# First block's rotary embedding: the halves of queries and keys exchanged by DMA within SBUF instead of by a matrix product

## The reference, cut to what matters

```
def apply_rope(x, cos, sin):
    x1, x2 = jnp.split(x.astype(jnp.float32), 2, axis=-1)
    ...
    return jnp.concatenate([x1 * c - x2 * s, x2 * c + x1 * s], axis=-1)

for l in range(DEPTH):                       # DEPTH = 2
    ...
    q = apply_rope(rms_norm(q.reshape(bsz, seq, 16, 64), q_norm_g[l]), cos, sin)
    k = apply_rope(rms_norm(k.reshape(bsz, seq, 16, 64), k_norm_g[l]), cos, sin)
    ...
    iq, ik = apply_rope(iq, cos, sin), apply_rope(ik, cos, sin)
    o_attn = dsa_attention(q, k, v, iq, ik, iw, n_keep) @ w_attn_o[l]
    xs, bm, cm = ...                         # convolution, state-space scan (ssd_scan), 32 heads
    ...
```

## Time and profile before

| What | Value |
|---|---|
| median of 3 runs | 2268.84 us (2265.83 to 2271.03) |
| the profiled execution's own time | 2264.96 us |
| its span, first to last instruction | 2263.2 us |
| TensorE busy | 2153.4 us, 95% of the span |
| VectorE busy | 1664.1 us, 74% |
| ScalarE busy | 1409.4 us, 62% |
| TensorE clock granted, mean | 0.993 of full speed |

### The profile page before, as it was taken

How to read it: one execution, slowest core, us unless ns; L and a number is a source line. 1 busy time by engine, 2 the same in 40 slices (tenths; PEclk the granted TensorE clock), 3 DMA queues, 4 the chain that set the end, 5 groups by cost and what they waited for, 6 DMA issues and landing times.

```text
span 2263.2 us, 42342 instructions
## 1 busy us (share of the span) xinstructions
PE 2153.4 (95%) x17416; PEld 2062.9 (91%) x17416; DVE 1664.1 (74%) x3018; ACT 1409.4 (62%) x2206; POOL 180.6 (8%) x170
## 2 busy tenths in 40 slices
PE   2989999999999899999999999899999999999999
PEld 1978899999999788999999999799999998899999
DVE  5898778678868987786678875757788784657654
ACT  2678897456546778974665456964654656764542
POOL 0000000022100000000124100000030110000000
PEclk9999999999999999999999999999999999999999
DMA  7545556657656555466565531545655422455663
GB/s 281 197 159 185 176 168 225 204 179 240 234 190 200 157 183 180 165 224 205 167 197 161 185 113 56 159 145 179 190 187 186 158 88 91 145 158 166 187 191 125
DMA packets 110593, 395.26 MB, mean 175 GB/s; under 512 B 12320, under 2 KB 13888, under 8 KB 110272
## 3 DMA queue, kind: packets, MB, share of 16 engines
q1 hardware_dynamic: 96768, 344.09, 47.1%
q0 software_dynamic: 11904, 43.03, 5.9%
q10 hardware_dynamic: 1728, 5.43, 0.6%
HBM read 391.46 MB, written 1.05 MB: 173 GB/s over the span
## 4 chain that ended last, share of the span: by engine, by line
PE 72%; ACT 12%; DVE 11%; issue 3%; DMA 2%; SPq 0%; ACTq 0%; DVEq 0%
PE bank L553 71%; ACT scr L1086 3%; ACT WH L1086 3%; DVE WL L1636 3%; ACT L1075 3%; ACT arena L1086 2%; DVE arena L1732 2%; DMA ring<-in_w 2%; DVE arena L2405 1%; DVE scr L1928 1%; DVE scr L1715 1%; DVE scr L1915 1%; DVE small L1927 0%; PE bank L637 0%; DVE scr L2001 0%
## 5 line engine op out<-in xcount | busy, mean ns | idle before, releaser
L1086 ACT ACTIVATE WH<-ring 128x1024 fp32r<-128x1024 f32 (+1 forms) x638 | 669.0, 1052 | 685.1 <-PE bank L553 660.7
L553 PE MATMUL bank<-HTH,WH 128*128 128x256 f32 (+1 forms) x3408 | 974.4, 286 | 13.5 <-DVE HTL L1705 4.7
L553 PE MATMUL bank<-HTL,WH 128*128 128x256 f32 (+1 forms) x3408 | 959.5, 282 | 0.0
L553 PE MATMUL bank<-HTH,WL 128*128 128x256 f32 (+1 forms) x3408 | 959.3, 281 | 0.0
L1636 DVE TENSOR_TENSOR WL<-ring,WH 128x1024 fp32r<-128x1024 f32 (+2 forms) x610 | 739.0, 1220 | 167.7 <-ACT WH L1086 165.0
L553 PEld LDWEIGHTS bank<-HTH,WH 128*128 128x128 f32 (+1 forms) x3408 | 643.3, 189 | 26.0 <-issue 7.8
L553 PEld LDWEIGHTS bank<-HTL,WH 128*128 128x128 f32 (+1 forms) x3408 | 643.4, 189 | 2.6 <-issue 2.1
L553 PEld LDWEIGHTS bank<-HTH,WL 128*128 128x128 f32 (+1 forms) x3408 | 643.2, 189 | 0.1
L1075 ACT ACT_TABLE_LOAD x119 | 152.7, 1283 | 22.1 <-DMA arena<-in_crow 13.4
L553 PE MATMUL bank<-ff2h,WH 128*128 128x256 f32 x512 | 143.8, 281 | 0.0
L553 PE MATMUL bank<-ff2l,WH 128*128 128x256 f32 x512 | 143.8, 281 | 0.0
(11 more groups left out here) (333 smaller groups left out, 3593.0 us busy)
## 6 DMA issues: line engine op xcount, KB each, us to landing
ring<-in_w SPq DMA_DIRECT2D x620, 512.0 KB, 4.1
arena<-in_wada POOLq DMA_DIRECT2D x80, 512.0 KB, 4.8
ring<-in_w SPq DMA_DIRECT2D x24, 384.0 KB, 3.3
arena<-in_wada SPq DMA_DIRECT2D x8, 512.0 KB, 19.2
arena<-in_wada ACTq DMA_DIRECT2D x8, 512.0 KB, 21.8
XT<-in_xt SPq DMA_DIRECT2D x1, 1024.0 KB, 9.0
arena<-in_s POOLq DMA_DIRECT2D x4, 256.0 KB, 3.7
ring<-in_w SPq DMA_DIRECT2D x8, 128.0 KB, 2.0
```

The source lines that it names most:

```text
L553: ins = e.matmul(out, a, b, start=(start and i == 0), stop=(stop and i == len(pairs) - 1))
L1086: return e.activation(out, a, func, **kw)
```

## The change

The permutation product of the eight rotary steps is gone from PE. Instead SP issues four DMAs for each of the eight, SBUF to SBUF: each moves a block of 32 partitions of queries and keys (2 rows of 512 fp32 in a partition, 128 KB) to the neighbouring block of 32 partitions in the lane's scratch tiles. SP issues them ahead of the load of the unit that lies 8 past the unit of step 11 or 22, after a wait on DVE's `gain`. DVE waits for all four and multiplies the scratch tiles in place. The sign goes from the matrix into the sine table (one more ACT instruction of 128x256 at the start); the permutation products of the indexer's queries and keys stay. The timetable changes: the step that takes up the exchanged halves comes three units after the gain and not two, and the steps behind it are one unit later until the next place where they meet the old numbers.

```diff
@@ timetable
-    "attn0": [5, 7, 9, 11, 13, 15, 17, 19, 21, 23, 25, 27, 29, 31, 33, 35, 39, 41, 43, 45, 47, 51, 53, 55, 57, 59, 61,
-              63, 65, 67, 69, 71],
-    "attn1": [5, 7, 9, 11, 13, 15, 18, 20, 22, 24, 31, 33, 35, 37, 39, 41, 43, 45, 47, 49, 51, 55, 57, 59, 61, 63, 65,
-              67, 69, 71, 73, 75],
+    "attn0": [5, 7, 9, 11, 13, 15, 17, 19, 21, 23, 25, 27, 30, 32, 34, 36, 39, 41, 43, 45, 47, 51, 53, 56, 58, 60, 62,
+              64, 66, 68, 70, 72],
+    "attn1": [5, 7, 9, 11, 13, 15, 18, 20, 22, 24, 31, 33, 36, 38, 40, 42, 44, 46, 48, 50, 52, 55, 57, 60, 62, 64, 66,
+              68, 70, 72, 74, 76],
@@ SyncE
+            exchanges = {plan.base[2 * l] + A_TICKS["attn%d" % par][slot] + 8: (l, par, bi)
+                         for l in range(2) for par in range(2) for bi, slot in ((par, 11), (par + 2, 22))}
             for x in units:
+                if x.i in exchanges:
+
+                    l, par, bi = exchanges[x.i]
+                    p.wait_ge((LA, LB)[par].V("gain", l, bi))
+                    for b in range(4):
+                        to, of = slice(32 * b, 32 * b + 32), slice(32 * (b ^ 1), 32 * (b ^ 1) + 32)
+                        e.dma_start(scr[to, 2 * par:2 * par + 2, :], QK[of, :, 512 * bi:512 * bi + 512]).then_inc(
+                            swapped[par].inc(*((l, bi) if b == 3 else ()), by=16), 16)
@@ TensorE
-                p.wait_ge(L.V("gain", l, bi))
-                mm(L.b[0][0:n, :], [(perm, xq)])
-                mm(L.b[1][0:n, :], [(perm, xk)]).then_inc(L.P.inc("turn", l, bi), 1)
@@ VectorE
-                p.wait_ge(L.P("turn", m, bi), L.V("gain", m, bi))
+                p.wait_ge(swapped[L is LB](m, bi), L.V("gain", m, bi))
                 for i, x in enumerate((xq, xk)):
-                    e.tensor_tensor(v2(s[i]), v2(b[i]), twice(sinap), ALU.mult).then_inc(L.V.inc(), 1)
+                    e.tensor_tensor(v2(s[i]), v2(s[i]), twice(sinap), ALU.mult).then_inc(L.V.inc(), 1)
@@ ScalarE, at the start
+            act(trig[:, 1, :], trig[:, 1, :], ACT.Identity, scale=con("sgn")).then_inc(start_scalar.inc(), 1)
```

More of the change, by code:

```diff
@@ L41 @@
 CONSTS = [("id", 128), ("ones", 128), ("blk", 128), ("perm", 128), ("dup", 64), ("tri0", 256),
-          ("mask", 256), ("rot", 256), ("scan", 256), ("invf", 1), ("eps", 1), ("same", 32)]
+          ("mask", 256), ("rot", 256), ("scan", 256), ("invf", 1), ("eps", 1), ("sgn", 1), ("same", 32)]
 def const_columns():
@@ L66, in const_array @@
         if m % 64 < 32:
-            put["perm"][m + 32, m] = -1
+            put["perm"][m + 32, m] = 1
         else:
@@ L83, in const_array @@
     put["eps"][:] = 1e-6
+    put["sgn"][:] = np.where(p % 64 < 32, -1, 1)
     return c
@@ L362, in program @@
         cst = sb("cst", [128, NCON])
-        cols = sb("cols", [128, NCOL + 30])
+        cols = sb("cols", [128, NCOL + 29])
         rows = sb("rows", [128, 128])
@@ L420, in program @@
         XCL, XCH = over("xcl", oXC, 16), over("xch", oK, 16)
+        QK = ar(0, 2, 2048)
         adabuf, silc = ar(oADA, 1024), ar(oSC, 1024)
@@ L476, in program @@
         opened = sig("opened")
+        swapped = [sig("swapped_a"), sig("swapped_b")]
         FREED_BY_VECTOR = {"su", "xc", "ao", "so", "res", "up", "pe", "b0", "b1", "b2"}
@@ L600, in attn @@
                 for bi in (par, par + 2):
-                    yield from rope_pe(L, l, bi, flat(Q[:, 2 * bi:2 * bi + 2, :]), flat(K[:, 2 * bi:2 * bi + 2, :]),
-                                       con("blk"), con("perm"), 128)
+                    yield
+                    p.wait_ge(L.A("sq", l, bi))
+                    mm(L.b[0][:, :], [(con("blk"), L.s[0])])
+                    mm(L.b[1][:, :], [(con("blk"), L.s[1])]).then_inc(L.P.inc("ss", l, bi), 1)
+                    yield
+                    yield
                     for pr in (2 * bi, 2 * bi + 1):
@@ L608, in attn @@
                                            lambda h, t: VV[:, t, 64 * h:64 * h + 64], ev_scalar("v", l, 3, 2 * l))
-            def rope_pe(L, l, bi, xq, xk, ones, perm, n):
-                yield
-                p.wait_ge(L.A("sq", l, bi))
-                mm(L.b[0][0:n, :], [(ones, L.s[0][0:n, :])])
-                mm(L.b[1][0:n, :], [(ones, L.s[1][0:n, :])]).then_inc(L.P.inc("ss", l, bi), 1)
-                yield
-                p.wait_ge(L.V("gain", l, bi))
-                mm(L.b[0][0:n, :], [(perm, xq)])
-                mm(L.b[1][0:n, :], [(perm, xk)]).then_inc(L.P.inc("turn", l, bi), 1)
-                yield
             def pair_pe(L, l, pr, before, bi, q, k, v, v_ready):
@@ L1594, in scalar_program @@
             p.wait_ge(start_vector("angle"))
-            act(trig[:, 1, :], x, ACT.Sin).then_inc(start_scalar.inc(), 1)
+            act(trig[:, 1, :], x, ACT.Sin).then_inc(start_scalar.inc("sine"), 1)
+            p.wait_ge(in_cst("in"), start_scalar("sine"))
+            act(trig[:, 1, :], trig[:, 1, :], ACT.Identity, scale=con("sgn")).then_inc(start_scalar.inc(), 1)
             act(y, x, ACT.Abs).then_inc(start_scalar.inc("abs"), 1)
@@ L1843, in rope_dve @@
             def rope_dve(L, m, bi, xq, xk, gq, gk, cosap, sinap, n):
-                s, b = [t[0:n, :] for t in L.s], [t[0:n, :] for t in L.b]
+                s = L.s
                 yield
```

## The result

The changed kernel is slower: median 2278.86 us (2275.97 to 2281.54, five executions) against 2268.84 us of the kernel before on the same chip (2265.83 to 2272.08), ratio 1.0043, 95% interval 1.0028 to 1.0057. Its profiled execution has a span of 2274.2 us, 11.0 us more than before; the granted clock is 0.989 on average, before 0.993. The forecast was 2264.4 us, a gain of 4.4 us.

A forecast was written before the change was run, and what follows sets the result against it. TensorE, busy 95% of the span, was taken to set the pace. A layer, 0.64 - 0.1 + 1.81 - 0.35 + 0.2 = 2.2 us, twice gives 4.4 of 14.7: 2268.84 - 4.4 = 2264.4 us, range 2256 to 2270.5.

The forecast's parts named there:

- fourth step: Units 59 to 62: wins of 1.72, 0.46 and 0.27 against a wait of 2.8, net -0.35 us a layer.
- pays 2.8: Unit 62: TensorE stands before `qk` at S + 6.9, keys come at S + 9.7, a 2.8 us wait.
- small waits that end: Units 64 to 76: attention in even units, scan in odd ones spreads ScalarE's work, winning 0.2 us a layer.
- first step: Unit 29: the scan's `y` needs VectorE's decays, so only 0.64 us come back and 1.3 become a wait.
- second step: Units 33 to 38: 1.1 us won, then lost to a 1.2 us wait for `attn1`'s keys; net -0.1 us.
- What is removed: Four permutation products a layer on TensorE: 7.35 us a layer, 14.7 for both, the most removal alone can give.
- Third step: Unit 55: no clump, `attn0` alone in unit 56, so the whole 1.81 us are won.
- Between and behind: Units 64 to 76, behind the fourth step: a win of 0.2 us a layer from small waits that end.
- second rival: Full ScalarE holds up even-unit steps, table changes in units 64 and 68: gain 0.4 us, 2268.4; chance 0.15.
- third rival: Late transfer, deciding from 8.5 us after the first step's gain; landing after 12 us gives 2273.6; chance 0.13.
- The Trainium skill's estimate: Exchange transfer: 1.3 + 2.0 + 2.4 = 5.7 us at half the ports, against 5.1 by the rows; hidden either way.
- forecast of 115 table loads: ScalarE's table loads fall by four in the new order, 5.1 us, to 115; not what the path waits for.

The follow-up runs named there:

- e1: The kernel before with only the new timetable, the permutation products staying on TensorE: 2281.17 us against 2267.80, ratio 1.0062.
- e14: The changed kernel with five idle products ahead of the wait for pair 6's keys in unit 62, a repeat run: 2272.57 us, ratio 1.0022.
- e9: Exchange by DMA on the old timetable with only the gains earlier, the first in unit 26: 2261.21 us against 2267.42 of the kernel before, ratio 0.9973.
- e10: The kernel before with an idle 64-column product ahead of each even unit from 38 to 74: 2295.06 us against 2267.42, ratio 1.0123.
- e2: The changed kernel without the 32 transfers and the wait for them: 2277.06 us, ratio 1.0042 to the kernel before.
- e5: The changed kernel with the old timetable, take-up two units after the gain: 2277.78 us, ratio 1.0048 to the kernel before.
- e13: The changed kernel measured once more, unaltered: 2278.46 us against 2267.99 of the kernel before, ratio 1.0039.
- e6: Exchange by DMA on the old timetable with only the gains one or two units earlier: 2261.42 us against 2266.89 of the kernel before, ratio 0.9979.
- e3: The changed kernel with attn0's steps from its probabilities on moved from units 60 to 72 to units 61 to 73: 2269.20 us, ratio 1.0004 to the kernel before.

## Why the prediction was wrong

The forecast was a gain of 2.2 us a layer; layer 0 lost 5.8, which is 8.0 us apart. **The step that failed first is the sum's last term of the fourth step, "pays 2.8"**: the wait came as forecast, but it was priced at its own length, and the lowered clock behind it took 2.7 us more in layer 0 and 1.5 in layer 1. Next is the term "small waits that end", a win of 0.2 where 1.8 were lost (2.0 of the 8.0), and 1.7 us for which the sum had no term. The other 1.6 are sizes: 1.0 in the first step, 0.2 in the second, 0.1 in the third, 0.3 in the fourth without its clock. The prediction weighed the removed products against single waits; it never added up what the new timetable costs by itself, and that is 13.4 us (e1).

By the prediction's own steps, layer 0, a minus being time won:

- **What is removed**: forecast 7.35 us. Comparing TensorE between the same rows of e1 and of the changed kernel, the four products are worth 1.72, 1.65, 1.72 and 1.70, in all 6.8. The rows of 1.91 held 0.2 that the 64-wide `y` behind needs in any case.
- **First step**: forecast -0.64. The wait for the decays came as forecast (1.3, measured 1.42), and the transfer's lateness added 0.70 at `qk`: 1.42 + 0.70 - 1.72 = +0.4.
- **Second step**: forecast +0.1; 1.27 + 0.65 - 1.65 = +0.3. The size was nearly right, the place not: I let `y` start at 183.5 without a wait, since ScalarE loses an Exp; it waited 1.27 as in unit 29. The wait for the keys was 0.65, half of the forecast.
- **Third step**: forecast -1.81, measured -1.72.
- **Fourth step**: forecast wait 2.8, measured 2.86. The chain was right link by link, not by luck. Waits alone: 2.86 + 0.22 - 0.46 - 0.27 - 1.70 = +0.65 (forecast +0.35). The lowered clock comes on top, +2.7; that it is the clock is shown by e14, where the wait is filled and the slow stretch gone. The trace of before already held such a fall, behind the 3.46 us before the scan's first `y`; the rows of the forecast begin at 160 us, behind it.
- **Between and behind**: forecast -0.2. `pt` of unit 50 waits 0.75 and that of unit 70 1.58, where before one wait of 0.53 stood: +1.8. The second rival ("everything is eaten", a table change to Exp in units 64 and 68) named the mechanism, at 1 us a time. ScalarE in order of time ahead of unit 70:

```profile
325.74 1.28 ACT L1080 ACT_TABLE_LOAD   x1
327.04 0.60 ACT L1091 ACTIVATE arena<-bank 128x512 f32<-128x512 f32 x1
327.65 1.28 ACT L1080 ACT_TABLE_LOAD   x1
328.95 0.40 ACT L1091 ACTIVATE scr<-scr,small 128x128 f32<-128x128 f32 x1
```

Two table loads of 1.28 us stand around one evacuation of 0.6 us, ahead of the Exp that `pt` hangs on.

The sum is 0.4 + 0.3 - 1.7 + 0.65 + 2.7 + 1.8 = +4.1 us (rounded); measured 5.8. In layer 1: -6.8 for the products, 7.55 for waits (8.82 come, 1.27 gone), 1.5 for the clock, +2.2; measured 3.9. About 1.7 us a layer stand in no row of a wait. e1, with the products kept, has 1.3 of them too: its residual rows of layer 0 start at 465.0, 5.9 us after those of before, and its TensorE was 0.7 us ahead of before at 152 us, in all 6.6, of which 5.3 are waits. e9, with the exchange and the old places of take-up, has none: its layer 1 is 3.7 us shorter than before (1086.4 - 455.3 against 1093.9 - 459.1 between the residual rows), which is the 6.8 of the products less 3.1 of new waits. So it belongs to the timetable. The pieces of 64-wide work that now stand alone fit this, at the 0.2 to 0.3 us of e10: I count three more of them between units 39 and 53, where some 0.8 us are lost without a wait. That they are the cause, and all of it, was not shown.

The third rival, a late transfer, was priced at "decides from 8.5 us": it landed after 9.3 and cost the 0.7 that this gives. It is not the cause here (e2), but it is in e5. The Trainium skill's estimate in the prediction, 5.7 us, and mine, 5.1, were both too low for the first step, where measured were 9.3 in the changed kernel and 7.4 in e5. They are not refuted for e9, where VectorE found the halves 5.8 us after the first issue and each of the four had landed within 2.3 to 2.6 us. The Trainium skill gives the fixed 2.0 us of that estimate, in "DMA: Bandwidth & Descriptors", Anatomy of one DMA, for transfers of the GpSimd path; these are issued by SP. What holds the first step's transfers up in one timetable and not in the other was not tested.

The forecast of 115 table loads was right and no argument: fewer of them in all, but a pair in the place that counts.

## What to carry to other kernels

A wait of an engine that sets the pace is worth more than its length when the clock falls behind it: price the slow stretch too, and look at the granted clock by stretch behind each of the longer waits, in the trace of before as well. When a transfer needs more time between two steps of a timetable, make its source earlier before making its user later: e9 and the changed kernel move the same halves in the same way, with as many units between, and 17 us lie between them. A new timetable is a change by itself: measure it alone first (e1). An operation that stands ahead of a waiting one is cover; removing it gives back only what the waited-for chain allows.

## What the hardware showed unexpectedly

- The clock's fall is not certain at a given wait, and its length varies. Behind the same 2.86 us the clock was low for some 6.8 us in layer 0 and 3.4 in layer 1 of the changed kernel, in e13 the other way round. Behind 1.63 us it fell in layer 0 of e9 and not in layer 1, and not in e6. Behind 2.15 us in e3 and 3.46 and 2.82 us in e1 it didn't fall at all.
- The scatter between executions goes with the clock: the kernel before took 2260.7 us at a mean clock of 0.995 and 2276.0 at 0.985, and in every kernel with five or more executions the slower ones have the lower mean clock.
- Issuing a transfer within SBUF over 32 partitions holds SP's queue for 0.59 us at least and up to 1.7 (e9), against 0.33 for a load of weights four times its size.
- VectorE's multiplication with both inputs in SBUF takes 687 ns on average and took 683 with one in PSUM: nothing is gained by leaving PSUM here.
